# Two convolution taps on ScalarE, the other taps placed anew, and another order of weights and products behind the output projection

## What is computed

```python
q, k, v, ca, cg = split(rmsnorm(h) @ w_in)                 # 512 columns each
z = q @ k.T / 8                                            # 8 heads, strictly causal
A[t,s] = sigmoid(z[t,s]) * prod(1 - sigmoid(z[t,j]) for j in s+1..t-1)
u = ca * sigmoid(cg)
conv = silu(layernorm(depthwise_conv31(u) + dw_b))         # 31 taps per channel
h = h + concat(A @ v, conv) @ w_out
h = h + (silu(rmsnorm(h) @ w_gate) * (rmsnorm(h) @ w_up)) @ w_down    # d_ff 2816
out = rmsnorm(h)[16:]
```

## Time and profile before

| | |
|---|---|
| median of 3 runs | 1206.67 us (1205.93 to 1207.23) |
| profiled execution, its own time | 1206.98 us |
| its span, first to last instruction | 1205.0 us |
| mean granted TensorE clock | 0.996 of 2.4 GHz |
| busy: PE, DVE, ACT, POOL | 1164.0, 690.3, 423.6, 483.6 us |

### The profile page before, as it was taken

One profiled execution on the slowest core, in us unless ns is written; L12 is line 12 of the kernel. 1 busy time (PEld: TensorE's weight loads), 2 busy tenths in 40 slices (PEclk: granted clock), 3 DMA queues, 4 the chain that ended last, 5 costly groups with the idle time before them and its releaser, 6 DMA issues.

```text
span 1205.0 us, 15351 instructions
## 1 busy us (share of the span) xinstructions
PE 1164.0 (97%) x5944; PEld 988.7 (82%) x5944; DVE 690.3 (57%) x752; ACT 423.6 (35%) x867; POOL 483.6 (40%) x370
## 2 busy tenths in 40 slices
PE   8999999999999899989999999999999999999997
PEld 6899799899898888867878788888888888878785
DVE  5349997987959755695343434343434343433347
ACT  6311452542636644453222222222222323131323
POOL 4115101301300012257646474737373738382822
PEclk9999999999999999999999999999999999999999
DMA  7203312203116011112121212121212121212113
GB/s 260 77 14 94 73 43 70 72 2 83 23 42 222 9 54 35 53 36 70 36 70 36 70 35 70 35 70 35 70 36 70 36 70 36 70 36 70 35 35 157
DMA packets 70911, 75.69 MB, mean 63 GB/s; under 512 B 11513, under 2 KB 60149, under 8 KB 70840
## 3 DMA queue, kind: packets, MB, share of 16 engines
q1 hardware_dynamic: 69656, 72.60, 19.6%
q10 hardware_dynamic: 1184, 2.13, 0.5%
HBM read 64.13 MB, written 6.32 MB: 58 GB/s over the span
## 4 chain that ended last, share of the span: by engine, by line
PE 61%; DVE 18%; POOL 12%; issue 8%; ACT 1%; DMA 0%; POOLq 0%; DVEq 0%; SPq 0%; ACTq 0%
PE ps L1816 20%; PE ps L1795 18%; DVE acc L1206 8%; PE ps L1600 8%; PE ps L1746 7%; DVE gq L1285 7%; PE ps L1557 4%; POOL wa_lo L643 4%; POOL wb_lo L643 2%; POOL wa_f L664 1%; POOL wa_f L658 1%; PE ps L1679 1%; POOL wa_f L661 1%; DVE qst L1185 1%; PE ps L1537 1%
## 5 line engine op out<-in xcount | busy, mean ns | idle before, releaser
L1467 DVE TENSOR_TENSOR mix<-ps,mix 128x512 f32<-128x512 f32 x176 | 121.7, 691 | 138.5 <-PE ps L1816 138.5
L1206 DVE SCALAR_TENSOR_TENSOR acc<-u_pad,par,acc 128x1024 f32<-128x1024 f32 x116 | 157.3, 1393 | 0.3
L1816 PE MATMUL ps<-wd_hi,act_hi 128*128 128x512 f32 x352 | 137.1, 389 | 1.4 <-DVE act_lo L1456 1.4
L1816 PE MATMUL ps<-wd_hi,act_lo 128*128 128x512 f32 x352 | 136.9, 389 | 0.0
L1816 PE MATMUL ps<-wd_lo,act_hi 128*128 128x512 f32 x352 | 136.9, 389 | 0.0
L643 POOL TENSOR_TENSOR wa_lo<-wa_f,wa_hi 128x512 fp32r<-128x512 f32 x58 | 79.3, 1370 | 132.3 <-ACT wa_hi L994 128.4
L585 POOL TENSOR_TENSOR wp_lo<-raw,wp_hi 128x1024 fp32r<-128x1024 f32 x16 | 52.1, 3254 | 197.5 <-ACT wp_hi L751 197.5
L1600 PE MATMUL ps<-hn_hi,wp_hi 128*128 128x348 f32 (+2 forms) x352 | 119.0, 338 | 3.1 <-DVE u_pad L1173 3.0
L1600 PE MATMUL ps<-hn_lo,wp_hi 128*128 128x348 f32 (+2 forms) x352 | 117.7, 334 | 0.0
L1600 PE MATMUL ps<-hn_hi,wp_lo 128*128 128x348 f32 (+2 forms) x352 | 117.5, 334 | 0.0
L1795 PE MATMUL ps<-t_hi,wa_hi 128*128 128x512 f32 x232 | 92.0, 396 | 6.6 <-POOL wa_lo L643 6.1
(11 more groups left out here) (187 smaller groups left out, 2622.8 us busy)
## 6 DMA issues: line engine op xcount, KB each, us to landing
raw<-in_w_gate SPq DMA_DIRECT2D x11, 1024.0 KB, 5.4
raw<-in_w_up SPq DMA_DIRECT2D x11, 1024.0 KB, 5.4
wd_f<-in_w_down SPq DMA_DIRECT2D x11, 1024.0 KB, 4.9
raw<-in_w_in SPq DMA_DIRECT2D x16, 512.0 KB, 3.9
xin<-in_x SPq DMA_DIRECT2D x8, 512.0 KB, 10.1
wo_raw<-in_w_out SPq DMA_DIRECT2D x4, 1024.0 KB, 8.7
mix<-in_x SPq DMA_DIRECT2D x8, 512.0 KB, 3.6
out<-ost SPq DMA_DIRECT2D x7, 512.0 KB, 2.6
```

Of the source, the lines that this page charges most:

```text
L1206: dve.scalar_tensor_tensor(out=acc[:, j % 2, :], in0=u, scalar=w, in1=acc[:, j % 2, :], op0=ALU.mult, op1=ALU.add).then_inc(conv_step, 1)
L1467: dve.tensor_tensor(hrow, ps[:, TB + n % 4, :], hrow, ALU.add).then_inc(d_added, 1)
L1816: last = pe.matmul(ps[:, TB + n % 4, :], a[s][:, t, i * P:(i + 1) * P], w_[m][:, t, dh * BANK:(dh + 1) * BANK], start=(t == 0 and s == m = ...
```

## The change

1. Taps 0 and 1 of each pair are made by ACT (`first_taps`, two activations with scale and bias per channel), between the two k splits of the pair before (for the first pair at the start). DVE's list of a pair is then 30 steps, `tap` for 2 to 30 and the addition (`STEPS` is 30).
2. DVE's steps are placed anew: 10 in place of 6 ahead of the first `glu` of a hand-over (in the first pair one ahead of it, beside the 23 of the start), 6 in place of 8 among the `glu`, 6 in place of 9 among the splits, 8 in place of 9 among the scans. For the last pair 10 more are made in the hand-over to it, so that 6 are left, 2 among the splits and 4 behind scans 8 to 11; `w_out`'s parts follow scans 12 to 15, and `spread` of the first corner stands ahead of the last scan. `step_values` of the last pair stands behind its second scan.
3. Behind the output projection: product (1, 2) has a load of its own too, its weight is made beside (1, 1)'s, and it is made directly behind (1, 1). The sum for product (0, 5) and its high part are made ahead of the last tile; the last `h_root` comes ahead of the sum for (0, 6). The sum, high and low part of (0, 7) move from the output projection's time to behind it. On DVE the two last T4 sums come behind T3's low part, on ACT T4's high part comes behind `weight_hi(1, 5)`.

```diff
-        FIRST_P = [(0, 1), (0, 2), (1, 1), (0, 3), (0, 5), (1, 2), (0, 6), (1, 5), (0, 7), (1, 6), (0, 4), (1, 7), (1, 3), (1, 4)]
-        FIRST_HI = [(0, 1), (0, 2), (1, 1), (0, 7), (0, 5), (0, 6), (0, 3), (0, 4), (1, 2), (1, 5), (1, 6), (1, 7), (1, 3), (1, 4)]
-        FIRST_LO = [(0, 1), (0, 2), (1, 1), (0, 7), (0, 3), (0, 5), (0, 4), (0, 6), (1, 2), (1, 5), (1, 6), (1, 7), (1, 3), (1, 4)]
-        FIRST_SLOT = [0, 1, 2, 0, 5, 2, 4, 0, 3, 5, 1, 2, 4, 3]
+        FIRST_P = [(0, 1), (0, 2), (1, 1), (1, 2), (0, 3), (0, 5), (0, 6), (1, 5), (0, 7), (1, 6), (0, 4), (1, 7), (1, 3), (1, 4)]
+        FIRST_HI = [(0, 1), (0, 2), (1, 1), (1, 2), (0, 5), (0, 6), (0, 3), (0, 4), (0, 7), (1, 5), (1, 6), (1, 7), (1, 3), (1, 4)]
+        FIRST_LO = [(0, 1), (0, 2), (1, 1), (1, 2), (0, 3), (0, 5), (0, 4), (0, 6), (0, 7), (1, 5), (1, 6), (1, 7), (1, 3), (1, 4)]
+        FIRST_SLOT = [2, 0, 1, 3, 2, 4, 5, 3, 0, 4, 1, 2, 5, 3]
...
             load_block(0)
-            sp.wait_ge(conv_step, past((CONV_K + 1) * PAIRS))
-            sp.dma_start(w_f_of(NTH[1, 1]), w_up_t[:, 0:KH, 0:P]).then_inc(fu_loaded, 16)
+            sp.wait_ge(conv_step, past(STEPS * PAIRS))
+            for k, ks in ((1, slice(0, KH)), (2, slice(KH, KD))):
+                sp.dma_start(w_f_of(NTH[1, k]), w_up_t[:, ks, 0:P]).then_inc(fu_loaded, 16)
...
+                if i == TILES - 1:
+                    pool.wait_ge(ms_used, TILES)
+                    weight_sum(0, 5)
                 if i >= 1:
                     h_root(i - 1)
                 if i == 3:
                     weight_lo(0, 1)
                     weight_lo(0, 2)
-                if i == 4:
-                    pool.wait_ge(conv_step, past((CONV_K + 1) * PAIRS))
-                    weight_sum(0, 7)
                 if i == 5:
                     up_first_lo(1)
-                    weight_lo(0, 7)
+                    up_first_lo(2)
+            h_root(TILES - 1)
             pool.wait_ge(wo_ready, 2 * TILES)
-            weight_sum(0, 5)
             weight_sum(0, 6)
-            h_root(TILES - 1)
             weight_sum(0, 3)
+            weight_sum(0, 7)
...
             weight_lo(0, 3)
             weight_lo(0, 5)
             weight_lo(0, 4)
             weight_lo(0, 6)
-            weight_lo(1, 2)
+            weight_lo(0, 7)
...
+            def first_taps(p):
+                if p == 0:
+                    act.wait_ge(u_zeroed, 1)
+                act.wait_ge(*freed("ca", 2, p))
+                act.wait_ge(conv_step, past(STEPS * p))
+                for j, bias in ((0, par[:, p, CONV_K:CONV_K + 1]), (1, zeros[:, 0:1])):
+                    act.activation(acc[:, j, :], u_pad[:, p % 2, j:j + L], ACT.Identity, scale=par[:, p, j:j + 1],
+                                   bias=bias).then_inc(conv_first, 1)
...
+            first_taps(0)
...
-                    for g in range(2):
-                        split_hi("k", g, p)
+                    split_hi("k", 0, p)
+                    first_taps(p + 1)
+                    split_hi("k", 1, p)
...
                 if i == 4:
                     up_first_hi(1)
-                    weight_hi(0, 7)
+                    up_first_hi(2)
                 if i + 1 < TILES:
                     ln_silu_of(i + 1)
                     mix_hi(i + 1, 1)
                 else:
                     act.wait_ge(ms_used, TILES)
+                    weight_hi(0, 5)
                     t_high("T1", 4, 6)
...
-            weight_hi(0, 5)
             weight_hi(0, 6)
             weight_hi(0, 3)
             evac_h(TILES - 1)
...
             weight_hi(0, 4)
             t_high("T1", 6, 8)
             copy(0, 1)
+            weight_hi(0, 7)
             t_high("T2", 6, 8)
-            weight_hi(1, 2)
             t_high("T3", 4, 8)
-            t_high("T4", 4, 8)
             silu(0, "C11")
             copy(0, 5)
             weight_hi(1, 5)
+            t_high("T4", 4, 8)
...
                 now, ahead = taps[p], taps[p + 1] if more else None
                 if more:
-                    some_taps(p, now, len(now) - 8)
                     if p:
+                        some_taps(p, now, 6)
                         spread(p - 1, 1)
-                    for g, n in zip(range(3), (3, 3, 2)):
+                    some_taps(p, now, len(now) - 6)
+                    for g, n in zip(range(3), (2, 2, 3)):
                         glu(g, p + 1)
                         some_taps(p, now, n)
                     assert not now
-                    for (kind, g), n in zip(GROUPS[6:10], (2, 3, 2, 2)):
+                    for (kind, g), n in zip(GROUPS[6:10], (1, 3, 2, 0)):
                         split_lo(kind, g, p)
                         if (kind, g) == ("k", 0):
                             step_values(p)
                         some_taps(p + 1, ahead, n)
                 else:
-                    for (kind, g), n in zip(GROUPS[8:10], (2, 1)):
+                    for (kind, g), n in zip(GROUPS[8:10], (2, 0)):
                         split_lo(kind, g, p)
                         some_taps(p, now, n)
-                    step_values(p)
                 for n, (h, i) in enumerate(UNITS):
                     w = width(i)
...
                     dve.tensor_tensor_scan(out=gates, data0=gates, data1=ones_row(w),
                                            initial=1.0, op0=ALU.mult, op1=ALU.mult).then_inc(scanned, 1)
                     if n == HELD_BACK - 1:
+                        if not more:
+                            step_values(p)
                         split_lo("q", 1, p)
-                    if more and (n < 2 or n > 8):
+                    if more and (n == 0 or n > 8):
                         some_taps(p + 1, ahead, 1)
-                    elif not more:
+                    elif not more and n > 6:
                         some_taps(p, now, 1)
-                    if not more and n >= WO_AT + 6:
-                        w_out_lo(n - WO_AT - 6)
+                    if not more and NU - 5 <= n < NU - 1:
+                        w_out_lo(n - NU + 5)
+                    if n == NU - 2 and not more:
+                        spread(p, 0)
                 assert more or not now
-                spread(p, 0)
+                if more:
+                    spread(p, 0)
                 if p + 2 == PAIRS:
-                    for g in range(2):
+                    for g, n in ((0, 3), (1, 3)):
+                        some_taps(p + 1, ahead, n)
                         split_lo("k", g, p + 1)
                     spread(p, 1)
+                    some_taps(p + 1, ahead, 4)
...
+            addition(0, "C11")
+            t_low(5, "T3", 4, 8)
             for i in (6, 7):
                 t_sum("T4", i)
-            addition(0, "C11")
-            t_low(5, "T3", 4, 8)
             addition(0, "U4")
...
             transpose_h(TILES - 1)
             pe.wait_ge(h_ready, 2 * TILES - 1)
             product(1, 1)
+            pe.wait_ge(h_ready, 2 * TILES)
+            product(1, 2)
             pe.wait_ge(hlo_ready, TILES)
             pe.wait_ge(ln_silu, 4 * TILES)
             product(0, 3)
             pe.wait_ge(tlo_ready, 2)
             product(0, 5)
-            pe.wait_ge(h_ready, 2 * TILES)
-            product(1, 2)
             pe.wait_ge(tlo_ready, 4)
             product(0, 6)
```

More of the change, by code:

```diff
@@ L46, in hybrid_block @@
     PAD = CONV_K - 1 - META
+    STEPS = CONV_K - 1
     IN_CORNER = P - META
@@ L339, in hybrid_block @@
         LO_NTH = {p_: n for n, p_ in enumerate(LO_ORDER)}
-        SLOT = FIRST_SLOT + [(0, 5, 1, 2, 4, 3)[n % SLOTS] for n in range(len(LATER))]
+        SLOT = FIRST_SLOT + [(0, 4, 1, 2, 5, 3)[n % SLOTS] for n in range(len(LATER))]
         def slot_freed(n):
@@ L371, in summed @@
         def summed(b, s_):
-            order = {0: ("S3", "S1", "S2", "S4"), 1: ("S1", "S2", "S3", "S4")}.get(b, ("S1", "S2", "S4", "S3"))
+            order = {1: ("S1", "S2", "S3", "S4")}.get(b, ("S1", "S2", "S4", "S3"))
             return 4 * b + order.index(s_) + 1
@@ L1012, in _ @@
                 if i == 2:
-                    act.wait_ge(conv_step, past((CONV_K + 1) * PAIRS))
+                    act.wait_ge(conv_step, past(STEPS * PAIRS))
                     weight_hi(0, 1)
@@ L1190, in tap @@
             def tap(p, j):
[L1192 removed]
+                base = STEPS * p
                 if j < CONV_K:
[L1194 to L1207 removed]
+                    if j < 4:
+                        dve.wait_ge(conv_first, 2 * p + j - 1)
+                    else:
+                        dve.wait_ge(conv_step, past(base + j - 3))
+                    dve.scalar_tensor_tensor(out=acc[:, j % 2, :], in0=u_pad[:, p % 2, j:j + L], scalar=par[:, p, j:j + 1],
+                                             in1=acc[:, j % 2, :], op0=ALU.mult, op1=ALU.add).then_inc(conv_step, 1)
                 else:
[L1209 removed]
+                    dve.wait_ge(conv_step, past(base + CONV_K - 2))
                     if p == 0:
@@ L1223, in _ @@
                 glu(g, 0)
```

(6 more changed lines are left out.)

22 lines of the change are left out of this document (3 added, 19 removed).

## The result

The changed kernel takes 1191.37 us (1191.04 to 1191.72, 4 runs) against 1206.82 us of the kernel before beside it, a ratio of 0.9873 (0.9856 to 0.989). That is the predicted 1191.3. But the two terms of the sum were not: attention gave 16.5 us where 11.9 stood, and the passage into the FFN lost 1.5 us where 3.5 were to be gained.

A forecast was written before the change was run, and what follows sets the result against it. PE, 97% busy, was taken as the bound, so only its idle or slow time could go: attention 11.9 us (11.2 - 0.5 + 1.2) plus passage 3.5 gave 15.4 us, hence 1191.3 us, range 1186.5 to 1198.5.

The forecast's parts named there:

- Attention, 11.2 us of waits: Attention: PE's 12.2 us of waits for DVE (scans, `glu`, corner tile) go, less 1.0 us allowed to stay.
- rival of 0.12: Whole kernel: pair-end waits go too and weight loads shorten, 18 us and a little more gained, 1188 or less; chance 0.12.
- The 1.0 us that I left: Attention, very end of pairs: waits behind scans that still have a tap between them, allowed 1.0 us for all.
- ACT, 0.5 us of new waits: Last pair: ACT, fuller with PE faster and `w_out` splits between copies, makes PE wait 0.5 us, between 0 and 2.
- The clock in the last pair, 1.2 us: Last pair's end, behind the corner's wait: PE's clock no longer falls, 12 matmuls gain 1.2 us, lower end 0.
- norm_h sooner, +0.9: Behind the output projection: `norm_h` starts about 1 us earlier, PE's wait for it falls from 1.24 to 0.3 us.
- (1, 2) in the gap, +2.6: Passage: product (1, 2) fills the 1.81 us wait for `lo_h`, and the 0.81 us ahead goes too; 2.6 us gained.
- The clock, +1.65: Passage: the 1.65 us lost to PE's clock of 0.97 over 55 us come back.
- New waits, up to -3.0: Passage: new or longer waits at (0, 6), (1, 5), (0, 7), (1, 6) cost 0.6 to 3.0 us.
- The strict reading of the Trainium skill's rule of the lock: Passage: DVE and POOL exclude each other fully, new waits cost the whole 3.0 us, so the passage gives 2.2 us.
- The fifth rival's threshold: Hand-overs: slower kernel if ACT's taps wait for DVE's addition, once it ends 4 us behind the first k group; chance 0.05.
- the likeliest case: Whole kernel: attention and passage gain as summed, 1188 to 1195 us; chance 0.61.

The follow-up runs named there:

- e8: Changed kernel with `spread` of the last pair's first corner put back behind the last scan; 1190.62 us, ratio 0.9879.
- e3: Kernel before with only taps 0 and 1 moved to ACT, all other DVE steps at their old places, passage as before; 1203.04 us, ratio 0.9975.
- e4: Changed kernel with taps 0 and 1 kept on DVE, ahead of tap 2 between the k splits, all else new; 1192.37 us, ratio 0.9879.
- e12: Changed kernel with three more activations of the same form on ACT ahead of each pair's two taps, each waiting for the one before; 1202.12 us, ratio 0.9976.
- e10: Kernel before with parts 1 and 2, and of part 3 only the sooner root, (0, 5)'s sum and high part, slots 4 and 5 exchanged; 1188.41 us, ratio 0.9862.
- e7: Changed kernel with product (1, 2) back behind (0, 5), its weight still made early; 1191.06 us, ratio 0.9881.
- e1: Kernel before with the attention half alone (parts 1 and 2), passage as before; 1190.27 us, ratio 0.9862.
- e11: As e10, with T4's new places on DVE and ACT as in the change; 1188.23 us, ratio 0.9864.
- e9: Changed kernel unaltered, run again in the third round beside the kernel before; 1189.62 us, ratio 0.9874.
- e5: Changed kernel with POOL's low part for (0, 7) moved behind the sums for (1, 5) and (1, 6); 1189.33 us, ratio 0.987.
- e6: As e5, with POOL also holding those sums and the low part until T2's low part is made; 1191.22 us, ratio 0.9883.

## Why the prediction was right, and where it was not

**The total was right because two errors cancelled:** 4.6 us too little for attention, 5.0 too much for the passage.

*Attention, 11.2 us of waits.* That these waits go was right, one by one, though the corner's goes with DVE's steps ahead of it and not with the place of `spread`, to which the prediction gave it (e8). The step that failed is the ledger itself: it counted the idle time in front of matmuls. From 134 us to the first mark PE's idle time fell by 11.8 us (14.15 to 2.38), and its busy time, for the same 2322 matmuls, by 4.7 (360.75 to 356.02). The waits view has a second set of rows, for weight loads, which the prediction named only in its rival of 0.12, without a row or a price. The kernel before and the changed one:

```profile
PEld ps L1664 <- DVE gq L1285: 10.2, 16, 1.8
...
PEld ps L1600 <- DVE u_pad L1173: 3.6, 2, 1.8
PEld ps L1619 <- DVE corner_w L1258: 2.1, 1, 2.1
```

```profile
PEld ps L1678 <- DVE gq L1292: 1.6, 4, 0.6
```

These are 15.9 - 1.6 = 14.3 us, against 12.2 - 0.4 = 11.8 by the matmuls' rows: 16 loads waited for scans, and only 11 matmuls have a wait. With 1.7 us for the clock that makes 16.0 of the 16.5. That a late load also makes the first matmuls behind it longer can be seen in single rows (0.50 us behind a wait in place of 0.39), but no run took this apart, so the match of the weight loads' rows is an agreement of numbers. A steady pair, with the clock at 1.00 in both kernels, agrees less closely: 84.32 us from its first scores to the next pair's before, 81.42 after, 2.9 us, where the matmuls' rows have 2.5 and the loads' rows 3.4 - 0.3 = 3.1.

*The 1.0 us that I left* for waits at pairs' ends did not stay: 0.4 is all.

*ACT, 0.5 us of new waits.* There were none; PE waits for nothing of ACT's in the last pair. DVE does: over the four pairs its scans wait 4.4 us for ACT's sigmoids, nothing before, and none of it reaches PE. DVE used the idle time of the hand-over to the last pair as forecast (5.64 us ahead of the q split became 0.86). A tap took 1.25 and 1.23 us by the groups view, above the 1.08 of my lower end:

```profile
L837 ACT ACTIVATE acc<-u_pad,par 128x1024 f32<-128x1024 f32 x4 | 5.0, 1248 | 13.0 <-issue 10.6 <-DVE mix L1219 2.4
L837 ACT ACTIVATE acc<-u_pad,zeros,par 128x1024 f32<-128x1024 f32 x4 | 4.9, 1228 | 0.0
```

The estimate of 1.2 us from the Trainium skill ("ScalarE: Activation LUTs", What ACT_TABLE_LOAD costs) agrees. Its advice to keep multiplications and additions on VectorE (Rules for kernel authors) is borne out here only so far: moving them was worth some 2.5 us with the old places (e3) and 0.1 with the new ones (e4), and it cost PE nothing because ACT had room, of which e12 shows 1.3 us a hand-over to be left.

*The clock in the last pair, 1.2 us.* It is 1.7; the earlier trace rows had it in the window's 0.96 of 46 us, which gives 1.8. I had priced 12 matmuls instead of the window. e3 shows that it does not need the waits to go: there the clock stayed at 1.00 behind the same waits.

*The passage: norm_h sooner, +0.9.* PE's wait fell as forecast (1.24 to 0.41 us). e10 shows that nothing is gained by it.

*(1, 2) in the gap, +2.6.* The gap was filled (1.81 to 0.21 us) and the work was missing at the next. This is the step that failed worst. I had counted a gap as PE's loss, where behind it a chain of other engines sets the time; e7 moves the product back and loses 0.5 us.

*The clock, +1.65.* It still fell in the changed kernel (0.97 over 56.5 us), which the prediction had named as a sign of being wrong. It costs next to nothing there: the clock over 500 to 560 us is 1.00 in e1 and 0.97 in e10, 0.94 in e11, with passages of 60.3, 60.6 and 60.1 us, and in e9, the changed kernel once more, it is 0.94 over 497 to 553.5 us with the same 62.0 us of passage. Where PE waits for others, slow matmuls eat into waits.

*New waits, up to -3.0.* Their places were named rightly: (0, 6) 4.29 us, (1, 6) 1.63, against 1.4 and 1.5 forecast. The second agreement does not repeat: in e9, the same kernel at the lower clock, PE waits only 0.29 us at (1, 6) and the passage is as long. (1, 5) and (0, 7), for which I had feared waits, had none, since they came behind the long one; (0, 5), with 0.87 us for T1's low part, was not on my list. What was mis-sized is (0, 6): I reckoned that one or two more of DVE's steps would be disturbed. The timelines of DVE and POOL after:

```profile
502.56 2.30 DVE L1351 SCALAR_TENSOR_TENSOR xn<-mix,rstd,g2b 128x1024 f32<-128x1024 f32 x1 [0.71 <-POOL rstd L579]
504.79 1.76 DVE L1370 TENSOR_TENSOR hn2f<-hn2f 128x512 f32<-128x512 f32 x1
506.47 1.78 DVE L1361 TENSOR_TENSOR b_lo<-hn2f,b_hi 128x512 fp32r<-128x512 f32 x1
...
513.27 2.31 DVE L1386 TENSOR_TENSOR t_lo<-hn2f,t_hi 128x1024 fp32r<-128x1024 f32 x1
...
518.40 4.50 DVE L1386 TENSOR_TENSOR t_lo<-hn2f,t_hi 128x1024 fp32r<-128x1024 f32 x2
```

```profile
512.76 1.74 POOL L646 TENSOR_TENSOR wb_lo<-wb_f,wb_hi 128x512 fp32r<-128x512 f32 x1
514.46 2.27 POOL L646 TENSOR_TENSOR wa_lo<-wa_f,wa_hi 128x512 fp32r<-128x512 f32 x1
518.20 1.41 POOL L661 TENSOR_TENSOR wa_f<-raw 128x512 f32<-128x512 f32 x1 [1.48 <-DMA raw<-in_w_up]
519.75 2.07 POOL L664 TENSOR_TENSOR wb_f<-wa_f,raw 128x512 f32<-128x512 f32 x1
```

One of DVE's steps before, undisturbed:

```profile
525.54 0.68 DVE L1356 TENSOR_TENSOR hn2f<-hn2f 128x512 f32<-128x512 f32 x1
```

From the start of `norm_h` to the end of T2's low part there are 20.3 us in place of 15.0 (519.92 to 534.89 before). Ten steps are disturbed in place of five, each by about 1.1 us: the two T2 parts take 4.50 us in place of 2.43. I had let POOL be done when they come; but the sum and the low part of (0, 7), which came in on POOL, delay DVE until its T2 parts stand beside the next block's sums. e5 shows it by moving one of the two away, which frees two of DVE's steps (1.77 us becomes 0.68, and 4.50 becomes 3.43), and e6 by holding back the two sums as well, which frees a third (2.43). The strict reading of the Trainium skill's rule of the lock ("SBUF — State Buffer", Who interferes with whom) came nearer than my count, with 2.2 us against 3.5, and was still 3.7 too high: the steps that stand side by side have to be counted along the chain, and neither did that.

*FFN.* Right: its chunks kept their length, and the shift is carried through.

*The fifth rival's threshold* (ACT 4 us late before PE notices) was wrong in kind: the DMA behind the high part of k is due sooner than the bank.

The range held; the likeliest case came out by its number and not by its reasons. Kept apart, the forecast of the halves would have been 11.9 with 7.5 to 13, and 3.5 with 2.2 to 4.6, and both fell outside.

**Open:** why e3 kept its clock; what late weight loads cost beyond the idle time in front of matmuls; whether the taps on ACT change the start; and how e11 would do on more runs. It is the fastest here by its median, 1.4 us below the changed kernel in the same round, and e1, the simplest, stands beside it by ratio (0.9862).

## What to carry to other kernels

Where an engine has idle time because others are late, add up its weight loads' waits and its busy time as well as the idle time in front of its matmuls, and read a clock's cost from the window; where it waits at several places in a row, first follow the chain behind the last of these places, because a gap filled ahead of that is only moved. Where VectorE and GpSimd share a stretch, count the steps of both on the chain: three of GpSimd's steps held back freed three of VectorE's here (e6), and one alone freed two (e5). Where the start varies by more than a term is worth, measure the term from a place behind the start. And when a total comes out right, measure its terms one by one before believing them.
